# The gated delta rule of a two-block kernel, its 16-blocks inverted by a recurrence on VectorE instead of squarings on TensorE, both head halves phase by phase

## The chip, the cores and the metric

One Trainium2 chip, one core of it. The metric is the device time of one launch in microseconds (us). TensorE, VectorE, ScalarE, GpSimd and SyncE appear in the rows as PE (its weight loads as PEld), DVE, ACT, POOL and SP (the queue of DMA issues as SPq). All data are fp32.

## The reference, cut to what matters

Two blocks run one after the other. The first (dilated attention, a convolution branch, memory attention, then a mixture of 32 experts over 256 tokens) matters here only through its experts, whose 192 MB of weights are read once. The second block projects 256 context tokens and 256 latent tokens, runs a state space scan (SSD) and a gated delta rule over both, in two directions, and ends in a feed-forward layer. The change is in the delta rule:

```python
def gdn_chunk_scan(q, k, v, log_a, beta, s0):
    """S_t = a_t (I - b_t k_t k_t^T) S_{t-1} + b_t k_t v_t^T, o_t = S_t^T q_t, chunked (WY form)."""
    g = jnp.cumsum(log_a, axis=2)
    diff = g[:, :, :, None] - g[:, :, None, :]
    a_mat = einsum("bclhd,bcshd->bclsh", k, k) * beta * masked_exp(diff, strict)
    lhs = a_mat + eye
    rhs = concatenate([v * beta, k * (beta * exp(g))], -1)
    u, w = split(triangular_solve(lhs, rhs, lower=True, unit_diagonal=True))
    qk = einsum("bclhd,bcshd->bchls", q, k) * masked_exp(diff, incl)
    def step(s, inp):
        v_new = u_c - w_c @ s
        o = (q * exp(g)) @ s + qk_c @ v_new
        s = s * dec_c + kd_c^T @ v_new          # kd = k * exp(g_last - g)
        return s, o
```

There are 8 heads of 128 channels. The kernel takes chunks of 128 tokens, so there are 2 chunks of context and 2 latent ones, in each direction: 8 chunk steps, and in each a 128x128 unit triangular matrix I + A per head has to be inverted.

## The kernel before, in words

**Stages.** The first block's attention part ends some 430 us into the span. Then the experts run (to some 1045 us), and on the same engines, woven in by a planned order, the second block's context part: its channels (projection, convolution), `ssd0` to `ssd3`, and the delta rule's context steps m = 0 to 3. After that come the latent channels, the SSD steps with the gate projections (some 1190 to 1299 us), the delta rule's latent steps m = 4 to 7 (`LATENT`, some 1297 to 1526 us), and the output projection and the feed-forward layer.

**The planner.** `context_phases` lists the context's phases with a cost each, `expert_phases` those of the experts, and `mixed_schedule` (L128) spreads the context's evenly over the experts' phases, in proportion to the costs (272.8 in all). Each engine's program is written in this order: an instruction of a later phase never passes one of an earlier phase on the same engine. The expert weights stream through a ring of 6 slots of 1 MB, issued by SP, which waits until the unit that held a slot has been used.

**One delta step before** (`gdn_pe` L561, `gdn_act` L941, `gdn_dve` L1174, `gdn_pool` L1523). The 8 heads are two halves h of 4. A "four" (L567 to L572) is one group of 4 fp32 products of 128x128x128 into one PSUM bank, written as 8 matmul instructions; `transposes` (L1966, the matmul at L1970) does 4 transposes the same way. In each phase the loop `for h in range(2)` does both halves:

- rows: transposes of k (gkT) and, as a four, the cumulated decay along the rows (gR); DVE clips the difference (L1190), ACT takes exp (L958, L961), POOL multiplies with the triangular mask (L1539, L1542);
- gram: k k^T (gKK, and on the latent side gQK); DVE multiplies (L1203) and cuts out minus the 16x16 diagonal blocks N (L1180); POOL adds the identity (L1547);
- AT: A transposed. P2, X2, X4, X8: (I + N)(I + N^2)(I + N^4)(I + N^8) by squarings, 8 fours per half, copied out of PSUM by ACT (L949) or added by DVE (L1222);
- three levels (blocks of 32, 64, 128): XT, T and Y, a transpose and two fours per half each, with POOL's masked copy of A (L1535) and DVE's subtraction (L1232);
- w (only where there is a state), v (L662, L664) and S: the state's part, the new values, outputs and the state.

**Around it.** `second_block_pe` (L797 to L809) puts the modulation products `mod_part` (L2123) and `mod_sum` (L785) and the sums `q_sums` (L792) between the phases; DVE does `modulate` (L1382), and after step 4 `gated_y` (L1390), after 5 `normed_y` (L1401). In the SSD steps the decays along rows come from fours (ssd_rows, L752), 4 per step.

## Time and profile before

| | before |
|---|---|
| runs | 1863.32, 1867.92, 1871.38 us; median 1867.92 |
| the profiled execution | 1869.31 us, its span 1867.6 us |
| PE busy | 1708.2 us (91%), mean granted clock 0.956 |
| DVE, ACT, POOL busy | 684.6, 435.7, 213.2 us |
| DMA | 372.69 MB, 200 GB/s over the span |

The span runs from the first to the last instruction of the profiled execution; its own time is 1.7 us longer. An engine's busy time counts neither its waits nor its semaphore instructions. TensorE's granted clock is a share of 2.4 GHz.

### The profile page before, as it was taken

How to read it: one execution, taken by the hardware profiler on the slowest of the kernel's cores; microseconds unless marked ns; L12 is line 12 of the kernel's file. 1: busy time of each engine (PE TensorE's matmuls, PEld its weight loads, DVE VectorE, ACT ScalarE, POOL GpSimd, SP SyncE). 2: the span in 40 equal slices, each digit the busy share in tenths (PEclk: the TensorE clock that was granted, in tenths of full speed). 3: DMA queues.
4: the chain of work that ended last, by engine and by line, in shares of the span. 5: the costliest groups of instructions: out<-in, count | busy, mean ns of one | idle time of the engine just before them, and what ended most of it. 6: DMA issues, size and time to landing. Idle time of an engine off the chain costs nothing.

```text
span 1867.6 us, 25449 instructions
## 1 busy us (share of the span) xinstructions
PE 1708.2 (91%) x10656; PEld 1209.9 (65%) x10656; DVE 684.6 (37%) x1404; ACT 435.7 (23%) x889; POOL 213.2 (11%) x190
## 2 busy tenths in 40 slices
PE   7999999999888879999999899899989989699996
PEld 3558555456666547767766588666978874488842
DVE  2107113335434353323233377665355450400003
ACT  1010454013111123323332231322333430000000
POOL 2000000020000012221212100011342320100000
PEclk9999999998988889999999899999999999799998
DMA  7444335723999888979989434224121222244340
GB/s 242 163 148 143 128 125 190 251 103 135 372 394 350 326 317 343 416 318 365 415 340 393 171 137 148 90 91 176 62 91 46 91 91 90 90 138 178 123 155 38
DMA packets 124295, 372.69 MB, mean 200 GB/s; under 512 B 10523, under 2 KB 26517, under 8 KB 107413
## 3 DMA queue, kind: packets, MB, share of 16 engines
q1 hardware_dynamic: 118245, 361.12, 51.6%
q0 software_dynamic: 1568, 8.39, 1.2%
q10 hardware_dynamic: 4368, 1.54, 0.4%
q8 instruction: 87, 1.43, 0.3%
q14 instruction: 27, 0.22, 0.0%
HBM read 369.98 MB, written 1.05 MB: 199 GB/s over the span
## 4 chain that ended last, share of the span: by engine, by line
PE 77%; DMA 13%; DVE 7%; ACT 1%; issue 1%; SPq 0%; DVEq 0%; ACTq 0%
PE psum L1976 49%; PE psum L571 10%; DMA ring<-in_w_down 4%; PE psum L1775 4%; DMA ring<-in_w_up 4%; DMA ring<-in_w_in 4%; PE psum L1970 3%; PE psum L1816 2%; PE psum L1759 2%; PE psum L1797 1%; PE psum L2093 1%; PE psum L768 1%; PE psum L2123 1%; PE psum L557 1%; DVE area L1180 1%
## 5 line engine op out<-in xcount | busy, mean ns | idle before, releaser
L1976 PE MATMUL psum<-area,ring 128*128 128x256 f32 x1984 | 457.7, 391 | 15.1 <-DMA ring<-in_w_in 14.1
L1976 PE MATMUL psum<-ring,area 128*128 128x512 f32 (+1 forms) x1040 | 452.5, 595 | 8.6 <-DMA ring<-in_w_proj_mem 2.4
L1976 PEld LDWEIGHTS psum<-area,ring 128*128 128x128 f32 x1984 | 386.1, 197 | 75.2 <-DMA ring<-in_w_in 18.1
L1976 PEld LDWEIGHTS psum<-ring,area 128*128 128x128 f32 x1040 | 198.9, 193 | 252.7 <-issue 251.7
L571 PEld LDWEIGHTS psum<-area 128*128 128x128 f32 x2304 | 269.7, 194 | 34.7 <-issue 19.1
L571 PE MATMUL psum<-area 128*128 128x128 f32 x2304 | 281.0, 280 | 10.6 <-DVE area L1180 10.4
L949 ACT ACTIVATE area<-psum 128x512 f32<-128x512 f32 x236 | 138.7, 597 | 243.7 <-PE psum L571 127.8
L2249 ACT ACTIVATE area<-psum 128x512 f32<-128x512 f32 x116 | 66.4, 599 | 460.9 <-PE psum L1976 362.2
L1970 PE MATMUL psum<-const,area 128*128 128x128 f32 x736 | 120.6, 294 | 52.0 <-DVE area L1490 14.8
L1970 PEld LDWEIGHTS psum<-const,area 128*128 128x128 f32 x736 | 90.5, 149 | 97.4 <-issue 23.0
L1775 PE MATMUL psum<-ring,area 128*32 128x256 f32 x2048 | 124.8, 388 | 12.5 <-DMA ring<-in_w_up 12.3
L1775 PEld LDWEIGHTS psum<-ring,area 128*32 128x32 f32 x2048 | 64.0, 111 | 59.3 <-issue 24.0
L1144 DVE SCALAR_TENSOR_TENSOR area<-area,cols 128x268 f32<-128x268 f32 (+1 forms) x186 | 91.6, 492 | 6.6
L1797 PE MATMUL psum<-ring,area 128*32 128x256 f32 x1024 | 68.2, 398 | 19.8 <-DMA ring<-in_w_down 19.4
L1535 POOL TENSOR_TENSOR area<-area,const 128x512 f32<-128x512 f32 x48 | 60.1, 1274 | 219.2 <-PE psum L571 219.2
L913 ACT COPY area<-psum 128x256 f32<-128x256 f32 x62 | 23.1, 373 | 210.6 <-PE psum L1976 210.6
L1142 DVE TENSOR_SCALAR area<-area,cols 128x268 f32<-128x268 f32 (+1 forms) x62 | 22.1, 356 | 120.3 <-ACT area L913 119.1
L1514 POOL TENSOR_TENSOR area<-area 128x1024 f32<-128x1024 f32 x4 | 10.8, 2728 | 461.9 <-DVE area L2371 461.9
L1797 PEld LDWEIGHTS psum<-ring,area 128*32 128x32 f32 x1024 | 31.0, 113 | 50.0 <-DMA ring<-in_w_down 22.0
L1501 DVE TENSOR_TENSOR area<-psum,area 128x512 f32<-128x512 f32 x11 | 7.6, 691 | 151.5 <-PE psum L1976 151.5
L1232 DVE TENSOR_TENSOR area<-area,psum 128x512 f32<-128x512 f32 x48 | 32.9, 687 | 67.2 <-PE psum L571 67.1
L1222 DVE TENSOR_TENSOR area<-psum,area 128x512 f32<-128x512 f32 x48 | 33.2, 691 | 60.7 <-PE psum L571 60.2
(304 smaller groups left out, 1346.5 us busy)
## 6 DMA issues: line engine op xcount, KB each, us to landing
ring<-in_w_gate SPq DMA_DIRECT2D x64, 1024.0 KB, 9.6
ring<-in_w_up SPq DMA_DIRECT2D x64, 1024.0 KB, 11.5
ring<-in_w_down SPq DMA_DIRECT2D x64, 1024.0 KB, 11.3
ring<-in_w_in SPq DMA_DIRECT2D x29, 2048.0 KB, 8.4
ring<-in_w_ada SPq DMA_DIRECT2D x12, 2048.0 KB, 8.1
ring<-in_w_in SPq DMA_DIRECT2D x13, 1024.0 KB, 7.5
ring<-in_w_out SPq DMA_DIRECT2D x6, 2048.0 KB, 8.5
ring<-in_w_ffn_gate SPq DMA_DIRECT2D x5, 2048.0 KB, 7.8
```

What stands on the lines that cost most here:

```text
L571: last = nc.tensor.matmul(dst[:, i * P:(i + 1) * P], lhs(i), rhs(i), start=True, stop=True)
L949: nc.scalar.activation(dst, src, ACT.Copy, scale=scale).then_inc(drain_of(key), 1)
L1144: link(v.scalar_tensor_tensor(dst, src, w, dst, ALU.mult, ALU.add))
L1222: v.tensor_tensor(bb[h][7], four(key), bb[h][7], ALU.add).then_inc(drain_of(key), 1)
L1535: g.tensor_tensor(b[6], b[3], by_row(LEVELS[lev]), ALU.mult).then_inc(s["level_ready"], 1)
L1759: last = nc.tensor.matmul(dst[:, j * P:(j + 1) * P], h2[:, t, k * P:(k + 1) * P], place[:, t, q * P:(q + 1) * P], start=t == 0, stop=t == ...
L1775: last = nc.tensor.matmul(wide.dst[CAP * j:CAP * (j + 1), 0:2 * P], hcT[:, q % 2, k, rows], both[:, :, k % 4, j * P:(j + 1) * P], start=k ...
L1797: last = nc.tensor.matmul(dst[CAP * g:CAP * (g + 1), 0:256], actT_e[:, e % 2, CAP * j:CAP * (j + 1)], w[:, j % 2, g * 256:(g + 1) * 256], ...
L1816: nc.tensor.matmul(dst, placeT[:, q, t * P:(t + 1) * P], y_quad[:, q % 2, half * WIDE:(half + 1) * WIDE], start=True, stop=True).then_inc( ...
L1970: last = nc.tensor.transpose(t[0:width, j * P:j * P + rows], src, ident[0:rows, 0:rows])
L1976: last = nc.tensor.matmul(dst, lhs(k), rhs(k), start=first and k == 0, stop=final and k == count - 1)
L2249: nc.scalar.activation(dst, src, func).then_inc(drain_of(key), 1)
```

## The change

Each half h is now a stream of its own (`gdn_pe(pe, m, h, ...)` and so on), and `staggered` weaves the two streams on every engine: with `STAGGER = 0` each phase of half 1 is followed at once by the same phase of half 0, which is emitted with it. The squarings go. In their place:

- compact (DVE): cut the 16x16 diagonal blocks out of A, fold them to 16 columns, spread them over (row, column) pairs;
- rep (PE, ACT): two products with the block mask, each with 512 columns, give each token all 256 entries of its own block for every head; ACT copies them out;
- solve (DVE): a recurrence of 15 steps, each a multiplication and a subtraction on 4 heads x n elements, n from 15 to 1, each instruction waiting for the one before; then four multiplications write the block-diagonal inverse, transposed, into XT;
- X0, Y0, X1, Y1, X2, Y2: one transpose and two fours per level as before, in two phases instead of three. AT is gone, since XT is kept transposed;
- where there is a state, w goes: k S (gK) is taken beside X2, scaled by ACT in 4 instructions and subtracted from beta v on DVE, and v is one four;
- gR, and ssd_rows of the SSD, are now transposes of the cumulated decay, not fours;
- the planner's costs are new (226.6 in all), and so is the place of the hooks for the modulation and the sums.

With the new costs the planner starts `rows 0` after `gate_up_b 14` (before: after `gate_up_a 12`), and the other steps after `down 17`, `down 21` and `turn 26` (before: `turn 16`, `down 20`, `gate_up_a 26`). Between `rep` and `X0` of both halves there stand, in the four context steps, `gate_up_b, down, turn`; `down, turn, gate_up_a`; `turn, gate_up_a, gate_up_b`; and `gate_up_a, gate_up_b`. Between `gram` and `rep` there are two of the experts' phases each time: `turn, gate_up_a`; `gate_up_a, gate_up_b`; `gate_up_b, down`; and `down, turn`.

```diff
 CTX_GAP = 3
+STAGGER = 0
...
+def staggered(first, second):
+
+    for _ in range(STAGGER):
+        yield "0 " + next(first)
+    while True:
+        phases = [("1 ", next(second, None)), ("0 ", next(first, None))]
+        if phases[0][1] is None:
+            return
+        for half, phase in phases:
+            if phase is not None:
+                yield half + phase
+
+
...
 
-    gdn = [("rows", 3.1), ("gram", 1.9), ("AT", 1.2), ("P2", 3.8), ("X2", 5.7), ("X4", 3.8), ("X8", 1.9), ("XT0", 1.2),
-           ("T0", 1.9), ("Y0", 1.9), ("XT1", 1.2), ("T1", 1.9), ("Y1", 1.9), ("XT2", 1.2), ("T2", 1.9), ("Y2", 1.9),
-           ("w", 1.9), ("v", 2.9), ("S", 1.9)]
+    costs = {"rows": 1.2, "gram": 1.0, "compact": 0.5, "rep": 1.8, "solve": 0.5, "X0": 1.6, "Y0": 1.0, "X1": 1.6, "Y1": 1.0,
+             "X2": 2.1, "Y2": 1.0, "v": 1.0, "S": 1.0}
...
+    half = [f"{name} {m}" for m in range(4) for name in costs]
+    return phases + [(phase, costs[phase.split()[1]]) for phase in staggered(iter(half), iter(half))]
...
+        def delta_half(h, wide, spread_at, columns, small_at):
+            triangle, keys, block, decay = [place + 512 * h for place in columns]
...
+                 [delta_half(h, 8192, 10240, (16000, 17024, 25216, 26240), 15360) for h in range(2)]]
+        unit_16 = stats[:, 24:40]
...
+            transposes(("gkT", m, h), [k_gdn[side][:, t, head * P:(head + 1) * P] for head in heads])
+            transposes(("gR", m, h), [cum[side][:, d, t, 16 + head:17 + head].to_broadcast([P, P]) for head in heads])
...
+            yield "compact"
+            pe.wait_ge(s["spread_ready"], 2 * m + h + 1)
+            for i in range(2):
+                pair = slice(2 * i, 2 * i + 2)
+                nc.tensor.matmul(open_tile(("gRep", m, h, i)), blk16, b["spread"][:, pair, :, :].rearrange("p h i j -> p (h i j)"),
+                                 start=True, stop=True).then_inc(filled, 1)
+            yield "rep"
+            yield "solve"
...
+                if lev == 0:
+                    pe.wait_ge(s["XT_ready"], 2 * m + h + 1)
+                else:
+                    wait_drained(pe, ("gY", m, h, lev - 1))
+                transposes(("gX", m, h, lev), [b["XT"][:, i, :] for i in range(4)])
+                pe.wait_ge(s[f"levels_{h}"], 3 * m + lev + 1)
+                four(("gV", m, h, lev), lambda i: b["AL"][:, i, :], lambda i: b["XT"][:, i, :])
+                if ci and lev == 2:
+                    wait_drained(pe, ("gS", m - 2, h))
+                    four(("gK", m, h), lambda i: b["kT"][:, i, :], lambda i: state[:, 4 * h + i, :])
+                yield f"X{lev}"
+                wait_drained(pe, ("gX", m, h, lev))
+                wait_drained(pe, ("gV", m, h, lev))
+                four(("gY", m, h, lev), lambda i: b["X"][:, i, :], lambda i: b["VT"][:, i, :])
...
+            wait_drained(pe, ("gY", m, h, 2))
             if ci:
...
+                pe.wait_ge(s["r_ready"], 2 * (m - 2) + h + 1)
+            else:
+                pe.wait_ge(s["kv_ready"], 2 * m + h + 1)
+            four(("gv", m, h), lambda i: b["XT"][:, i, :], lambda i: b["A"][:, i, :])
...
+        def gdn_steps(steps, half):
+
+            def of_half(h):
+                for m in steps:
+                    for phase in half(m, h):
+                        yield f"{phase} {m}"
+
+            return staggered(of_half(0), of_half(1))
...
                     dst = open_tile(("ssd_rows", m, q))
                     for j in range(4):
-                        last = nc.tensor.matmul(dst[:, j * P:(j + 1) * P],
-                                                log_a[1][:, c - 2, d, 4 * q + j:4 * q + j + 1].to_broadcast([P, P]),
-                                                (upto, since)[d], start=True, stop=True)
+                        last = nc.tensor.transpose(dst[:, j * P:(j + 1) * P],
+                                                   cum[1][:, d, c - 2, 4 * q + j:4 * q + j + 1].to_broadcast([P, P]), ident)
                     last.then_inc(filled, 1)
...
+            for phase in gdn_steps(LATENT, lambda m, h: gdn_pe(pe, m, h, open_tile, transposes)):
+                half, phase, m = phase[0], phase[2:-2], int(phase[-1])
                 tile = MOD_FIRST + 2 * (m - 4)
-                for phase in gdn_pe(pe, m, open_tile, transposes):
+                if half == "0":
                     if phase == "gram":
                         mod_part(tile)
-                    if phase == "AT":
+                    if phase == "rep":
                         mod_sum(tile)
-                    if phase == "X8":
+                    if phase == "X0":
                         mod_part(tile + 1)
-                    if phase == "T1":
+                    if phase == "X2":
                         mod_sum(tile + 1)
-                if m in (5, 6):
...
+            for i in range(2):
+                key = ("gRep", m, h, i)
+                nc.scalar.copy(b["rep"][:, 2 * i:2 * i + 2, :, :].rearrange("p h i j -> p (h i j)"),
+                               wait_filled(eng, key)).then_inc(drain_of(key), 1)
...
-            yield "AT"
-            yield "P2"
-            for name in ("X2", "X4", "X8"):
-                for h in range(2):
-                    key = ("g" + name, m, h)
-                    v.tensor_tensor(bb[h][7], four(key), bb[h][7], ALU.add).then_inc(drain_of(key), 1)
-                yield name
-            yield "XT0"
+            wait_drained(eng, ("gKK", m, h))
+            block, rows = b["block"], b["rows"]
+            link(v.tensor_tensor(block, b["A"], blk16.unsqueeze(1).to_broadcast([P, 4, P]), ALU.mult))
+            link(v.tensor_reduce(rows, block.rearrange("p h (g j) -> p h j g", j=16), AX.X, ALU.add))
+            for i in range(4):
+                ins = v.tensor_tensor(b["spread"][:, i, :, :], rows[:, i, :].unsqueeze(1).to_broadcast([P, 16, 16]),
+                                      unit_16.unsqueeze(2).to_broadcast([P, 16, 16]), ALU.mult)
+            ins.then_inc(s["spread_ready"], 1)
+            yield "compact"
+            yield "rep"
+            rep, Y, tmp = b["rep"], b["Y"], b["step"]
+            link(v.tensor_copy(Y, unit_16.unsqueeze(1).to_broadcast([P, 4, 16])))
+            for i in range(2):
+                wait_drained(eng, ("gRep", m, h, i))
+            for j in (range(15), range(15, 0, -1))[d]:
+                left = (slice(j + 1, 16), slice(0, j))[d]
+                n = left.stop - left.start
+                link(v.tensor_tensor(tmp[:, :, 0:n], rep[:, :, left, j], Y[:, :, j:j + 1].to_broadcast([P, 4, n]), ALU.mult))
+                link(v.tensor_tensor(Y[:, :, left], Y[:, :, left], tmp[:, :, 0:n], ALU.subtract))
+            XT = b["XT"]
+            for i in range(4):
+                ins = v.tensor_tensor(b["XT"][:, i, :].rearrange("p (g j) -> p g j", j=16),
+                                      Y[:, i, :].unsqueeze(1).to_broadcast([P, 8, 16]),
+                                      blk16.rearrange("p (g j) -> p g j", j=16), ALU.mult)
+            ins.then_inc(s["XT_ready"], 1)
+            yield "solve"
             for lev in range(3):
-                yield f"T{lev}"
-                for h in range(2):
-                    key = ("gY", m, h, lev)
-                    if lev == 2:
-                        wait_drained(eng, ("gXT", m, h, lev))
-                    dst = bb[h][7 if lev < 2 else 4]
-                    v.tensor_tensor(dst, dst, four(key), ALU.subtract).then_inc(drain_of(key), 1)
+                yield f"X{lev}"
+                key = ("gY", m, h, lev)
+                v.tensor_tensor(XT, XT, four(key), ALU.subtract).then_inc(drain_of(key), 1)
+                if ci and lev == 2:
+                    wait_drained(eng, ("gK", m, h))
+                    eng.wait_ge(s["kv_ready"], 2 * m + h + 1)
+                    v.tensor_tensor(b["A"], b["A"], b["AL"], ALU.subtract).then_inc(s["r_ready"], 1)
                 yield f"Y{lev}"
-                if lev < 2:
-                    yield f"XT{lev + 1}"
-            if ci:
...
+                wait_filled(eng, ("gRep", m, h, 1) if lev == 0 else ("gV", m, h, lev - 1))
+                g.tensor_tensor(b["AL"], b["A"], by_row(LEVELS[lev]), ALU.mult).then_inc(s[f"levels_{h}"], 1)
```

## Rows read from the trace of the kernel before

**Rows 1.** the page: busy time of each engine over the span.

```profile
PE 1708.2 (91%) x10656; PEld 1209.9 (65%) x10656; DVE 684.6 (37%) x1404; ACT 435.7 (23%) x889; POOL 213.2 (11%) x190
```

**Rows 2.** the page: the chain that ended last, by engine.

```profile
PE 77%; DMA 13%; DVE 7%; ACT 1%; issue 1%; SPq 0%; DVEq 0%; ACTq 0%
```

**Rows 3.** busy us by stretch, four experts in each, beside context steps.

```profile
core 0: us, PE busy (x) PEld busy (x) DVE busy (x) ACT busy (x) POOL busy (x), PEclk, DMA share, GB/s
722.20:792.20 70.00, 65.99 (x711) 50.09 (x710) 25.22 (x49) 23.37 (x46) 17.40 (x14) 0.98 0.92 372
792.20:859.40 67.20, 63.12 (x703) 48.17 (x702) 18.64 (x35) 19.40 (x40) 11.56 (x10) 1.00 0.86 349
859.40:927.30 67.90, 65.25 (x718) 49.58 (x718) 21.76 (x46) 23.18 (x47) 20.21 (x16) 1.00 0.95 380
927.30:998.00 70.70, 66.75 (x734) 51.63 (x733) 23.68 (x51) 23.96 (x46) 14.41 (x11) 1.00 0.91 365
sum 275.80, PE 261.11 PEld 199.48 DVE 89.31 ACT 89.92 POOL 63.59; mean PE 65.28 PEld 49.87 DVE 22.33 ACT 22.48 POOL 15.90
```

**Rows 4.** two stretches of 10 us among the experts, columns as above.

```profile
750.00:760.00 10.00, 10.00 (x127) 7.46 (x129) 2.52 (x5) 4.34 (x10) 5.88 (x6) 1.00 1.02 418
800.00:810.00 10.00, 10.00 (x139) 7.58 (x138) 1.73 (x5) 2.70 (x6) 0.00 (x0) 1.00 0.24 78
```

**Rows 5.** the two parts of latent step 5, columns as above.

```profile
1357.84:1368.70 10.86, 3.86 (x10) 1.97 (x10) 10.86 (x31) 4.19 (x7) 7.81 (x6) 0.69 0.57 194
1368.70:1411.60 42.90, 42.39 (x362) 39.55 (x362) 13.57 (x21) 17.46 (x29) 15.89 (x13) 1.00 0.15 50
```

**Rows 6.** the page, groups: busy us, mean ns | idle before, releaser.

```profile
L571 PE MATMUL psum<-area 128*128 128x128 f32 x2304 | 281.0, 280 | 10.6 <-DVE area L1180 10.4
...
L1232 DVE TENSOR_TENSOR area<-area,psum 128x512 f32<-128x512 f32 x48 | 32.9, 687 | 67.2 <-PE psum L571 67.1
```

**Rows 7.** timeline of PE among the experts: start us, us, engine, line.

```profile
732.74 1.93 PE L1775 MATMUL psum<-ring,area 128*32 128x256 f32 x32
734.61 2.05 PE L571 MATMUL psum<-area 128*128 128x128 f32 x16
...
745.17 0.66 PE L1970 MATMUL psum<-const,area 128*128 128x128 f32 x4
...
792.05 3.74 PE L1759 MATMUL psum<-area 128*128 128x128 f32 x32
795.62 3.60 PE L1816 MATMUL psum<-area 128*128 128x512 f32 x8
```

**Rows 8.** timeline of latent step 5, clips to gram, columns as above.

```profile
1357.84 4.22 DVE L1190 TENSOR_SCALAR area<-psum,area 128x128 f32<-128x128 f32 x16
...
1359.69 2.49 POOL L1539 TENSOR_TENSOR area<-area,const 128x512 f32<-128x512 f32 x2 [18.54 <-ACT area L958]
...
1361.97 2.15 DVE L1203 SCALAR_TENSOR_TENSOR area<-psum,area 128x128 f32<-128x128 f32 x8
...
1363.14 2.15 PE L1970 MATMUL psum<-const,area 128*128 128x128 f32 x8 [5.38 <-DVE area L1203]
...
1365.09 1.92 PE L785 MATMUL psum<-area 128*128 128x512 f32 x2
```

**Rows 9.** timeline of DVE in the router, a chain of linked small instructions.

```profile
424.10 0.17 DVE L2639 TENSOR_TENSOR area<-area,r_prio 128x16 f32<-128x16 f32 x1
424.30 0.17 DVE L2640 TENSOR_REDUCE area<-area 128x2 f32<-128x16 f32 x1
...
432.77 0.23 DVE L2684 SCALAR_TENSOR_TENSOR area<-area 128x64 f32<-128x64 f32 x1
```

**Rows 10.** a group of DVE by shape: busy us, mean ns | idle before.

```profile
L2541 DVE TENSOR_TENSOR area<-area 128x256 f32<-128x256 f32 x6 | 2.5, 424 | 0.2
```

**Rows 11.** line L752, the SSD decays: ns min/median/max.

```profile
L752 PE MATMUL psum<-const,area x128: 275/275/276, 1187.7 to 1274.5; 128*128 128x128 f32 x128
```

**Rows 12.** line L1180 of DVE: ns min/median/max.

```profile
L1180 DVE SCALAR_TENSOR_TENSOR area<-area,const x32: 677/684/1774, 705.8 to 1485.7; 128x512 f32<-128x512 f32 x32
```

More of the change, by code:

```diff
@@ L1570, in gdn_pool @@
[L1570 to L1578 removed]
+            yield "compact"
+            yield "rep"
+            wait_drained(eng, ("gKK", m, h))
@@ L1597, in context_pool @@
                 yield f"ssd{m}"
[L1598 to L1600 removed]
+            for phase in gdn_steps(range(4), lambda m, h: gdn_pool(eng, g, m, h)):
+                yield phase
         def experts_pool():
```

450 lines of the change are left out of this document (153 added, 297 removed).

## The prediction, made before the changed kernel was run

> **What bounds the kernel now.** I read the page first: PE is busy nine tenths of the span [rows 1], and PE makes up 77% of the chain that ended last, DMA 13%, DVE 7% [rows 2]. So removed products count only where nothing else then ends last. The delta rule runs in two places.
>
> Among the experts, four experts and about one context step take 70.0, 67.2, 67.9 and 70.7 us, 275.8 together; PE is busy 261.1 of them and the DMA share is 0.86 to 0.95 [rows 3]. In a 10 us stretch the DMA moves 418 GB/s where it is never held up, and 78 GB/s beside a gather and scatter, where PE uses no weights [rows 4]. Four experts are 4 x 6 units of 1 MB, 25.2 MB, or 60.2 us at 418 GB/s. Both resources are close: PE ends last, but 4 x 60.2 = 241 us is the floor that no saving on PE goes below, 35 us under today's 276.
>
> On the latent side nothing streams worth speaking of. Step 5 has two parts: 10.9 us in which DVE is busy throughout and PE for 3.9, then 42.9 us in which PE is busy for 42.4 [rows 5]. From the first clip to the last product of S that is 53.8 us.
>
> **What leaves PE.** A four costs 0.89 us (1.95 us for 16 instructions with the first one's latency, 280 ns each before overlap [rows 6]; two fours stand as 2.05, two gathers' worth of 32 instructions as 3.74 [rows 7]). A group of transposes costs 0.55 in a row of them (0.66 alone [rows 7]). Per half, a context step has 18 fours (20 with a state) and 5 groups of transposes; afterwards 9 (10), 5 groups (gR takes AT's place) and the two 512-column products of rep. Such a product stands as 1.02 us alone (two instructions, 1.92 at the low clock [rows 8]); in a row I take 0.90 each, 1.8 per half, nearly two fours. Net 7 (8) fours, 6.2 (7.1) us per half, so 12.5, 12.5, 14.2 and 14.2 us per context step: **53 us less PE work among the experts**. The same on the latent side.
>
> **What DVE adds.** All of it is in series with PE, because X0 of a half waits for its XT.
> - compact, per half: a multiplication and a fold over 512 elements (0.69 each [rows 6]) and four multiplications of 256 (424 ns alone [rows 10], about 1.47 for four back to back): 2.9 us.
> - solve, per half: 30 linked instructions on 4 to 60 elements, 32 on average. A linked pair on 16 elements starts 0.20 us apart and 64 elements take 0.23 [rows 9]; I take 0.22, between them, and keep 0.20 and 0.26 as ends. 30 x 0.22 = 6.6, a copy 0.2, four multiplications into XT 1.1 (as 16 clips of 128 take 4.22 [rows 8]): 7.9 us (7.3 to 9.1).
> - Both halves: 5.8 us of compact and 16.0 us (waits included) of solve per step, in place of squarings that PE did while ACT and DVE followed at 0.3 us.
>
> **The latent steps.** STAGGER is 0, so between rep and X0 PE has nothing of the other half; only `mod_sum` stands there. From the first clip: clips 4.2, then gram of half 1 (1.1 and 0.6), gram of half 0 when POOL's masks (1.25 each, now A, QK, A, QK [rows 8]) let it: 7.7 us. Compact to 13.5. Rep and its copies of half 1 are done by then. Solve of half 1 to 21.6, of half 0 to 29.6. X0 of half 1 is hidden in this, that of half 0 is not. After it PE runs: X0 1.4, mod_part 1.9, Y0 1.8, X1 2.9, Y1 1.8, X2 with gK 4.7, mod_sum 1.0, Y2 1.8, two subtractions exposed 1.0 (0.69 each [rows 6]), v 3.6, S 3.6: 25.5, in all 55.1 against 53.8, **+1.3 us per step** at full clock. But after its 5 us of idleness at 1357.84 the granted clock of that stretch is 0.69 [rows 5] and the next products come at 1.92 instead of 1.02 us [rows 8]: that is the lower of the two levels, 1.2 GHz. Now PE is idle for about 6 us before rep and some 12 of the 16 us of solve, so I let rep (which pushes solve by 1.2) and X0 with mod_part (+1.4 and +1) run at that level: +3.6, less 0.9 for what step 5 already loses so today. **+4 per step, +16 us for four** (low end 4 x 1.3 = 5; high end 4 x 5 = 20, with 0.26 per link 30).
>
> Work of DVE between the steps (gated_y, normed_y, the sums) stays where it was and costs the same. The hooks on half 1's X0 stand where DVE waits for Y0 anyhow; if that cover went, `o_squares` would cost 3 us once.
>
> **The context steps.** Per step PE waits twice. At rep: DVE needs 2.1 + 2.9 us for half 1 and 2.9 more for half 0, the experts' phases in between fill 2 to 4 us (1.93 each [rows 7]): about 3 us of waiting. At X0: between rep's end and X0 three phases fill about 4 us; solve of half 1 ends 7 us after rep, of half 0 another 8 later; X0 of half 1 is 1.5 of it: 3 + 6.7 = 9.7 us of waiting. Together 12.8 us, and 1.5 for restarting at the low clock: 14.3 x 4 = 57 us. Behind solve on DVE stands the experts' multiplication out of PSUM, and behind that on PE the turn and `down`, and behind those SP's loads: it costs no more as long as PE waits at X0 anyway. The ring holds 6 MB, 15 us at 418 GB/s, so DMA goes on during such a wait and takes 5 of the 14.7 us (275.8 - 261.1 [rows 3]) that PE waits today. Where the planner puts phases sums to nothing: the channels spread over more experts, the delta steps are denser later. **-53 + 57 - 5 = -1 us.** The bounds are far: -25 if the waits fall where PE would wait for weights, +25 if all that PE idles today stays and links cost 0.26.
>
> **The SSD steps.** 16 fours of L752 (275 ns, 128 instructions [rows 11]) become transposes, 16 x 0.34 = **-5 us**, since PE is the busy one there; 0 if DVE ends last instead.
>
> gK's scaling on ACT, POOL's products and the reduction into unit_16 cost nothing: each runs while PE or DVE is busy with the other half; without that cover gK's four activations would cost 1.2 us in each of four steps.
>
> **The sum.** -1 - 5 + 16 = +10 us. Against the profiled execution's 1869.3 that is 1879.3; the median stands 1.4 lower, so 1878.
>
> **The rivals.**
> 1. *The experts gain after all* (0.31), the other side. Place: the stretches of rows 3. Price: a wait at X0 costs nothing while PE would soon stand before an empty ring. For it: weights land late at many points even now, and DMA has 35 us to give. Against: PE waits only 14.7 us there today. It decides once the waits per step are under about 8 us: then the experts' part gains 25, the latent steps with their low end cost 8: 1869 - 25 - 5 + 8 = 1847, less the 1.4: 1846.
> 2. *It comes out even* (0.08): the clock is kept through solve, latent +5, nothing among the experts: 1868.
> 3. *POOL in DVE's way* (0.09). The clearest row is L1180: two SBUF inputs, 684 ns as a rule, 1774 at most, beside POOL's masks [rows 12]. All of solve's instructions have two SBUF inputs, and POOL's level masks for both halves run as soon as rep is filled, 1.25 us each, beside compact of half 0 and solve of half 1. If they exclude each other that is 2.5 us per step, 8 x 2.5 = 20 us: 1898. The Trainium skill states such a rule ("SBUF — State Buffer", Who interferes with whom): a VectorE instruction with two inputs in SBUF and a GpSimd instruction that reads SBUF take the shared read port by turns, each for its whole length. By that rule, which the stretched row agrees with, rival 3 would be the right size or a bit under it.
> 4. *The ring starves* (0.05): DVE late for the experts, waits beyond the ring's 15 us: another 30 us, 1908.
> The forecast keeps 0.47; its own range is 1862 to 1898.
>
> **The numbers.** 0.5% is 9.3 us, about what this kernel's measurements can tell. Faster by more: rival 1 but for 0.04, 0.27. Slower by more: the forecast but for 0.07, and rivals 3 and 4, 0.54. Within: 0.19. The range runs from rival 1 to rival 4.
>
> **What would show it.** Right: PE idle before X0's transposes, put down to DVE, 7 to 10 us per step among the experts and 6 + 7 us on the latent side; a granted clock well under 1 there; steps 4 to 6 from clip to S near 58 us; the four stretches near 69 us still. Wrong: stretches near 62 us and a DMA share near 1 (rival 1); links 0.3 us apart or more beside POOL (rival 3); DVE's solve much shorter than 7.9 us per half, in which case all of this shrinks.

## The result, and the profile after

| | before | after |
|---|---|---|
| median (range), runs | 1865.62 us (1862.92 to 1871.38), 4 | 1980.87 us (1977.35 to 1985.16), 4 |
| ratio after / before | | 1.0614, 95% interval 1.0577 to 1.0651 |
| span of the profiled execution | 1867.6 us | 1977.0 us |
| mean granted clock | 0.956 | 0.914 |

The change costs 6.1%. The forecast had the sign, and a tenth of the size. Of the page after, first the busy times [rows 1], the chain [rows 2], and the groups that wait most [rows 6]:

```profile
PE 1610.7 (81%) x9408; PEld 1093.7 (55%) x9408; DVE 797.9 (40%) x1993; ACT 402.6 (20%) x862; POOL 174.9 (9%) x162
...
PE 68%; DVE 15%; DMA 10%; ACT 3%; issue 2%; POOL 1%; SPq 0%; DVEq 0%; ACTq 0%; POOLq 0%
...
L1909 PE MATMUL psum<-const,area 128*128 128x128 f32 x736 | 125.6, 302 | 156.7 <-DVE area L1186 119.0
L592 PE MATMUL psum<-area 128*128 128x128 f32 x1408 | 192.2, 293 | 27.0 <-ACT area L923 19.9
...
L608 PE MATMUL psum<-area,const 128*128 128x512 f32 x64 | 47.7, 915 | 59.6 <-DVE area L1170 59.6
```

PE is busy 97.5 us less (111 were expected: 53, 53 and 5), DVE 113.3 more, and DVE's share of the chain has doubled. PE stands 119.0 us before X0's transposes (L1909, released by the writes into XT, L1186) and 59.6 before rep (L608, released by compact's last multiplication, L1170).

**Where the time went.** Three marks that both kernels have cut the span: the first of the latent channel products (the experts' end), the first clip of latent step 4, and the first output product after step 7. Busy us of each engine from the first gather (L1759 before, L1698 in the changed kernel) to the experts' end, and over the latent steps, before:

```profile
core 0: us, PE busy (x) PEld busy (x) DVE busy (x) ACT busy (x) POOL busy (x), PEclk, DMA share, GB/s
438.24:1061.14 622.90, 553.27 (x5328) 400.57 (x5326) 228.55 (x479) 166.99 (x377) 87.42 (x64) 0.94 0.88 345
1295.58:1542.73 247.15, 219.80 (x1791) 196.42 (x1791) 127.31 (x245) 93.79 (x158) 88.45 (x74) 0.96 0.25 91
```

and after, the same columns, with the three stretches of four experts that answer to those of [rows 3]:

```profile
434.86:1112.90 678.04, 507.74 (x4752) 347.56 (x4750) 285.25 (x771) 151.02 (x358) 68.24 (x52) 0.88 0.80 317
1344.31:1653.52 309.21, 179.08 (x1191) 143.38 (x1190) 183.57 (x541) 77.54 (x152) 69.25 (x58) 0.80 0.20 74
...
708.23:804.77 96.54, 62.43 (x586) 39.77 (x584) 49.10 (x138) 21.49 (x40) 19.46 (x14) 0.84 0.62 247
804.77:888.91 84.14, 60.41 (x622) 42.38 (x621) 37.95 (x123) 20.59 (x41) 14.20 (x12) 0.86 0.75 299
888.91:969.15 80.24, 61.76 (x638) 44.21 (x637) 39.35 (x123) 22.29 (x47) 14.23 (x12) 0.89 0.85 335
```

The span's +109.4 us are: experts' end 1112.9 against 1061.1, **+51.8**; from there to the first latent clip 231.4 against 234.4, **-3.0** (the SSD's part); the latent steps, **+62.1**; the rest **-1.4**. (From the first gather on the experts' part is 55.1 longer; it starts 3.4 earlier.) Among the experts PE's busy time fell by 45.5 and its idle time rose by 100.7 (69.6 to 170.3); on the latent side busy fell by 40.7 and idle rose by 102.8 (27.4 to 130.1). The forecast had 52 (57 - 5) and 69 (16 + 53): so the rise is twice as large among the experts and half as large again on the latent side.

**What PE waits for.** Latent step 6, clip at 1423.53, the timeline of after: start us, us, engine, line, in brackets the idle time before it and its releaser.

```profile
1423.53 4.22 DVE L1146 TENSOR_SCALAR area<-psum,area 128x128 f32<-128x128 f32 x16
1426.74 0.63 ACT L930 ACTIVATE area<-area 128x512 f32<-128x512 f32 x1 [10.33 <-DVE area L1146]
...
1428.42 3.58 PE L592 MATMUL psum<-area 128*128 128x128 f32 x16 [9.53 <-ACT area L923]
...
1439.33 0.68 DVE L1167 TENSOR_TENSOR area<-area,const 128x512 f32<-128x512 f32 x1
1440.05 1.00 DVE L1168 TENSOR_REDUCE area<-area 128x64 f32<-128x512 f32 x1
1441.08 1.43 DVE L1170 TENSOR_TENSOR area<-area,stats 128x256 f32<-128x256 f32 x4
...
1442.57 6.73 PE L608 MATMUL psum<-area,const 128*128 128x512 f32 x8 [8.72 <-DVE area L1170]
...
1449.45 1.26 POOL L1495 TENSOR_TENSOR area<-area,const 128x512 f32<-128x512 f32 x1 [1.69 <-PE psum L608]
1449.46 1.32 DVE L1183 TENSOR_TENSOR area<-area 128x48 f32<-128x48 f32 x1
1450.81 0.23 DVE L1182 TENSOR_TENSOR area<-area 128x44 f32<-128x44 f32 x1
1451.07 0.20 DVE L1183 TENSOR_TENSOR area<-area 128x44 f32<-128x44 f32 x1
...
1455.73 0.90 DVE L1186 TENSOR_TENSOR area<-area,const 128x128 f32<-128x128 f32 x4
...
1463.80 0.90 DVE L1186 TENSOR_TENSOR area<-area,const 128x128 f32<-128x128 f32 x4
...
1464.75 1.11 PE L1909 MATMUL psum<-const,area 128*128 128x128 f32 x4 [14.59 <-DVE area L1186]
```

Half 1 has its spread at 1439.4, but rep of half 1 begins at 1442.57, when half 0 has its own too. Half 1 has its XT at 1456.6, but its X0 begins at 1464.75, when half 0's is done. The exp of half 1 (L930) starts when half 0's first four clips are done too. PE has nothing of one half to do beside the other's solve. The code gives a reason: the waits on signals (semaphores) that both halves share count `2 * m + h + 1` (L605, for one), the value at which half 0 and then half 1 have signalled; `staggered` emits half 1 first, and its wait for `2 * m + 2` is met only by half 0. Twelve waits have this form. That is a reading of code and rows; the first two runs below test it.

The links, the small instructions of solve that wait for one another, run as forecast where nothing disturbs them (0.17 to 0.25 us each, starts 0.20 to 0.28 apart).

### The profile page after: what moved, and what is told of

It is laid out like the page before. It is cut to its first block, busy times and chain, and to the rows that moved or that the text cites. A ratio compares the mean times of both kernels' runs of the same rounds, so it can differ in the third digit from the quotient of the medians.

```text
span 1977.0 us, 23427 instructions
## 1 busy us (share of the span) xinstructions
PE 1610.7 (81%) x9408; PEld 1093.7 (55%) x9408; DVE 797.9 (40%) x1993; ACT 402.6 (20%) x862; POOL 174.9 (9%) x162
## 3 DMA queue, kind: packets, MB, share of 16 engines
q8 instruction: 77, 1.26, 0.3%
## 4 chain that ended last, share of the span: by engine, by line
PE 68%; DVE 15%; DMA 10%; ACT 3%; issue 2%; POOL 1%; SPq 0%; DVEq 0%; ACTq 0%; POOLq 0%
PE psum L1915 45%; PE psum L592 7%; PE psum L1909 3%; PE psum L1714 3%; DMA ring<-in_w_up 3%; DMA ring<-in_w_in 3%; DMA ring<-in_w_down 3%; DVE area L1182 3%; DVE area L1183 3%; PE psum L608 2%; PE psum L1736 2%; PE psum L1755 1%; PE psum L1698 1%; DVE area L1170 1%; POOL area L1498 1%
## 5 line engine op out<-in xcount | busy, mean ns | idle before, releaser
L1915 PE MATMUL psum<-area,ring 128*128 128x256 f32 x1984 | 448.5, 386 | 10.3 <-DMA ring<-in_w_in 9.3
L1909 PE MATMUL psum<-const,area 128*128 128x128 f32 x736 | 125.6, 302 | 156.7 <-DVE area L1186 119.0
L592 PE MATMUL psum<-area 128*128 128x128 f32 x1408 | 192.2, 293 | 27.0 <-ACT area L923 19.9
L1909 PEld LDWEIGHTS psum<-const,area 128*128 128x128 f32 x736 | 96.9, 155 | 197.2 <-DVE area L1186 123.9
L592 PEld LDWEIGHTS psum<-area 128*128 128x128 f32 x1408 | 181.7, 207 | 43.3 <-issue 22.1
L2188 ACT ACTIVATE area<-psum 128x512 f32<-128x512 f32 x116 | 66.4, 599 | 455.4 <-PE psum L1915 359.5
L923 ACT COPY area<-psum 128x512 f32<-128x512 f32 x128 | 73.4, 588 | 231.8 <-PE psum L1909 168.6
L1714 PEld LDWEIGHTS psum<-ring,area 128*32 128x32 f32 x2048 | 67.3, 115 | 84.8 <-issue 52.2
L608 PE MATMUL psum<-area,const 128*128 128x512 f32 x64 | 47.7, 915 | 59.6 <-DVE area L1170 59.6
L1495 POOL TENSOR_TENSOR area<-area,const 128x512 f32<-128x512 f32 x48 | 61.2, 1274 | 313.0 <-PE psum L592 199.8
L1463 DVE TENSOR_TENSOR area<-psum,area 128x512 f32<-128x512 f32 x11 | 7.6, 692 | 151.0 <-PE psum L1915 151.0
L608 PEld LDWEIGHTS psum<-area,const 128*128 128x128 f32 x64 | 18.4, 303 | 87.0 <-DVE area L1170 64.9
L1182 DVE TENSOR_TENSOR area<-area 128x60 f32<-128x60 f32 (+14 forms) x240 | 52.7, 220 | 33.4 <-ACT area L939 25.4
L1194 DVE TENSOR_TENSOR area<-area,psum 128x512 f32<-128x512 f32 x48 | 32.9, 687 | 69.5 <-PE psum L592 68.8
```

The lines of the kernel that those rows point to most:

```text
L592: last = nc.tensor.matmul(dst[:, i * P:(i + 1) * P], lhs(i), rhs(i), start=True, stop=True)
L608: nc.tensor.matmul(open_tile(("gRep", m, h, i)), blk16, b["spread"][:, pair, :, :].rearrange("p h i j -> p (h i j)"), start=True, stop=Tru ...
L923: nc.scalar.copy(dst, src).then_inc(drain_of(key), 1)
L1182: link(v.tensor_tensor(tmp[:, :, 0:n], rep[:, :, left, j], Y[:, :, j:j + 1].to_broadcast([P, 4, n]), ALU.mult))
L1495: g.tensor_tensor(b["AL"], b["A"], by_row(LEVELS[lev]), ALU.mult).then_inc(s[f"levels_{h}"], 1)
L1714: last = nc.tensor.matmul(wide.dst[CAP * j:CAP * (j + 1), 0:2 * P], hcT[:, q % 2, k, rows], both[:, :, k % 4, j * P:(j + 1) * P], start=k ...
```

## The experiments

All ratios are to the kernel before, run beside each kernel on the same chip. Differences in us are of medians of different sets of runs, between which before's own median moved from 1864.83 to 1869.33; so they are good to some 5 us, and where that matters the ratios are compared too. "Solve" and "rep" are the phases, "after" is the changed kernel, and "the swapped order" the first run.

**1 and 2. The order of the halves, and the counts.** The first swaps what `staggered` emits, the second leaves it and makes the waits count in the order of emission, in 12 places:

```diff
-        phases = [("1 ", next(second, None)), ("0 ", next(first, None))]
+        phases = [("0 ", next(first, None)), ("1 ", next(second, None))]
```
```diff
-            pe.wait_ge(s["spread_ready"], 2 * m + h + 1)
+            pe.wait_ge(s["spread_ready"], 2 * m + 2 - h)
```

> The changed kernel with half 0 emitted ahead of half 1 in every phase (one line of `staggered`). Theory A: the waits count 2m+h+1, as if half 0 signalled first; with half 1 emitted first, half 1's waits ask for both halves (2m+2), so rep, X0 and the masks of half 1 wait for half 0's work too. Then this order lets the first half go ahead: in the latent steps gram is done some 5 us earlier, rep of the first half 3 us earlier and X0 of it is hidden in the second solve: clip to S falls from 70.6 us to 57 to 60, and the wait before X0 among the experts from 17 to about 10. Whole kernel 1895 to 1925 us. Rival B (length of the recurrence and low clock alone, order indifferent): within 8 us of the changed kernel's 1981.

> The changed kernel, half 1 still first, but the twelve waits of the form 2m+h+1 count in the order of emission (2m+2-h). Theory A: the same gain as with half 0 first, within 8 us of that run, 1895 to 1925 us, since only the counts coupled the halves. Rival B: 1981 within 8. If the order itself matters (hooks, POOL's order) and not the counts, this stays near 1981 while the other order gains.

Measured: 1923.05 us, ratio 1.0277 (1.0245 to 1.0309), and 1924.57 us, ratio 1.0298 (1.0251 to 1.0345). Two different edits, one effect: 56 to 58 us of the 115 by the medians, 59 to 63 by the ratios. In the first, PE's waits from 430 to 1620 us (in total, how often, the longest), and latent step 5:

```profile
PE psum L1909 <- DVE area L1186: 95.4, 16, 9.2
PE psum L608 <- DVE area L1170: 28.3, 11, 4.3
```
```profile
1417.22 1.88 PE L758 MATMUL psum<-area 128*128 128x512 f32 x2
1423.57 1.11 PE L1909 MATMUL psum<-const,area 128*128 128x128 f32 x4 [4.47 <-DVE area L1186]
...
1432.72 1.12 PE L1909 MATMUL psum<-const,area 128*128 128x128 f32 x4 [6.33 <-DVE area L1186]
```

X0 now waits 16 times (once per half and step) and at most 9.2 us, instead of 8 times and at most 17.3 in after; X0 of half 0 starts 9.15 us before that of half 1, beside its solve. Latent falls from 309.2 to 268.6 us, the experts' end from 1112.9 to 1099.4. The coupling is shown, and it is mostly a matter of the latent side. The rest of the runs build on the swapped order where not said otherwise.

**3 and 9. A short solve.** One of the recurrence's 15 steps is left, so the inverted blocks aren't those of the reference; the third run has after's order, the ninth the swapped one.

```diff
-            for j in (range(15), range(15, 0, -1))[d]:
+            for j in (range(14, 15), range(1, 0, -1))[d]:
```

> The changed kernel with 1 of the 15 steps of the recurrence left in each solve (the other 14 are left out, so the block inverses are not the reference's). 28 linked DVE instructions, 6.2 us, less per half, 16 halves: 100 us less on DVE. If solve is exposed in full: 1981 - 100 = 1881. Where the ring or the experts' weights would have ended last among the experts, less comes back there: the latent half (8 halves) 50 us, the experts' part 30 to 50: 1881 to 1901. If the coupling and not the length of solve were the whole of the loss: under 40 us gained.

> Half 0 first, as in the run that changed only that, and 1 of the recurrence's 15 steps left, so the inverted blocks are not those of the reference. About 12.5 us of DVE per half-pair and step go, 100 us in all. Theory A (with the halves uncoupled, solve's length is still what PE stands for): PE's waits at X0, 95 us, nearly vanish; experts lose most of the 52 us that context steps wait, latent falls from 268.6 to some 225: 1830 to 1850, below before. Theory B (what is left of the loss sits in the low clock, in compact and in the order of the phases): the waits move to other places, and it stays at 1865 or above.

Measured: 1874.22 us, ratio 1.0025 (1.0001 to 1.0049), so 107 under after; and 1816.50 us, ratio 0.9723 (0.9674 to 0.9773), 107 under the swapped order. The ninth kernel's stretches, first gather to experts' end and latent:

```profile
435.38:1051.40 616.02, 507.02 (x4752) 342.79 (x4750) 241.57 (x547) 150.58 (x358) 68.35 (x52) 0.91 0.88 349
1283.54:1489.99 206.45, 164.13 (x1192) 131.80 (x1190) 138.29 (x317) 78.36 (x152) 70.49 (x58) 0.93 0.30 110
```

Against the swapped order DVE is busy 102 us less (810.8 to 708.9). Solve's length, the gaps between its links included, falls by 117, from 145 us in all to 28, half of it in each part. The time falls by 107 us by the medians, with the halves coupled or not (110 with them coupled and 103 without by the ratios): by 62.2 on the latent side, but by 48.0 among the experts, where waits for weights take back a part (the section on the prediction has the rows). So nearly the whole length of solve was exposed. Both runs came out below what was expected of them. With next to no solve the new form would be 2.8% faster than before, and most of that is latent (206.5 us instead of 247.2); the experts' part, 616.0 instead of 622.9, gains 6.9 us of the 46 by which PE's busy time fell.

**4 and 5. The low clock.** Products whose result nobody reads keep PE busy before rep and X0: in the fourth run on after's latent side alone, in the fifth in all steps of the swapped order.

```diff
                         mod_sum(tile)
+                        for _ in range(13):
+                            nc.tensor.matmul(psum[:, 6, :], ones, const[:, 0:4, :].rearrange("p a n -> p (a n)"), start=True, stop=True)
```

(and 5 of them behind `mod_part` in the fourth run; in the fifth 1 and 2 before rep of half 0 and 1, and 4 and 6 before X0).

> The changed kernel with extra products on constants in PE's idle time of the latent steps: 5 of 512 columns before rep (after mod_part), 13 between rep and X0 (after mod_sum); results unused. Clock theory: rep (6.7 us at the low level for four products) falls towards 4 and X0 to Y0 lose their 2 to 3 us: 4 to 5 us per step, 1961 to 1965 in all. Rival: the idle time was never worth more than 1 us per step, 1977 to 1981. If the extra products run into X0, up to 10 us slower.

> The kernel with half 0 first, and extra products of 512 columns on constants in the PSUM bank that is written next: 1 and 2 before rep, 4 and 6 before X0 of half 0 and 1, in all eight steps (results overwritten). They stand where PE waits for DVE. Clock theory: between gathers PE is busy 61 to 62 us where before it was 65 with some 13 us more work, so the low level costs 8 to 9 us per step among the experts and 3 on the latent side; kept at the full level that comes back: 1923 - 30 = 1893 (range 1880 to 1905). Rival (the waits cost by their length alone, and the extra products only get in the way where the wait is short): 1920 to 1935.

Measured: 1983.92 us, ratio 1.0592 (1.0551 to 1.0634), the latent part 308.5 us, no gain; and 1914.55 us, ratio 1.0264 (1.0236 to 1.0291), 8.5 under the swapped order. The fourth kernel's step 6:

```profile
1449.47 5.21 PE L608 MATMUL psum<-area,const 128*128 128x512 f32 x8 [4.07 <-DVE area L1176]
1454.51 1.02 PE L758 MATMUL psum<-area 128*128 128x512 f32 x2
1455.38 11.32 PE L783 MATMUL psum<-const 128*128 128x512 f32 x26
1471.20 1.11 PE L1915 MATMUL psum<-const,area 128*128 128x128 f32 x4 [4.51 <-DVE area L1192]
```

Rep shrank from 6.73 to 5.21 us, but the idle products (L783) ended 4.5 us early and X0 ran at the lower level all the same, so this run says nothing of X0. The fifth does: its stretches of four experts stand at a granted clock of 0.92, 0.96 and 1.00 (the swapped order's 0.87, 0.89, 0.89), its latent part at 0.92 instead of 0.82. The gain is small and uncertain: 8.5 us by the medians, about 2 by the ratios, whose intervals overlap, 11.4 by the profiled spans (the experts' end is 10.0 earlier, the latent part 3.2 shorter). So holding the clock in this way gives back 2 to 11 us, not the 30 that were expected. What the low clock costs by itself isn't separated, since the idle products can also hold up PE's own work (run 12).

**6. The planner's cost of solve**, 6.3 instead of 0.5, so that more of the experts' phases stand between rep and X0.

> The kernel with half 0 first and the planner's cost of solve 6.3 instead of 0.5 per half, so that the context's total is as large as before and some six of the experts' phases stand between solve and X0. If PE's wait for XT among the experts (about 10 us per step) is a matter of too little work beside it, it goes, and the channels are as dense as before: 1923 - 25 to 35 = 1888 to 1898. Rival: the experts' multiplication stands behind solve on DVE, in order, so PE stops at the experts' turn instead of at X0: 1910 to 1930, with the wait moved to other lines.

Measured: 1901.08 us, ratio 1.0190 (1.0161 to 1.0218), 22 us under the swapped order by the medians, 16 by the ratios, and all of it among the experts (end at 1074.5, latent 268.5). PE's wait at X0 fell from 95.4 to 46.8 us, which is the latent side's alone; part of it came back elsewhere, for DVE works in order: the experts' turn waits 20.2 us for DVE's multiplication (L1865), which is written behind a solve.

**7. The transposes alone**: the kernel before with gR and ssd_rows as transposes.

> The kernel before with one part of the change alone: gR and ssd_rows as transposes of the cumulated decay. The prediction's term: 5 us less in the SSD steps, 0.3 us per half in the delta steps, where gR runs under DVE's work: 1869 - 5 = 1864 (0.3% faster), and 1859 if gR's saving among the experts counts too. Rival: nothing, DVE ends last there: ratio 1.000.

Measured: 1862.44 us, ratio 0.9981 (0.9963 to 0.9998), 2.4 us faster; the part from the experts' end to the first latent clip is 232.4 instead of 234.4.

**8. Half 0 six phases ahead**, `STAGGER = 6` in after; this also puts the signals into the order that the counts ask for.

> The changed kernel with STAGGER 6 instead of 0: half 0 is six phases ahead of half 1, so the solve of one half stands beside v, S, rows and gram or X0 to Y2 of the other, and half 0 signals first, as the counts ask. If the loss is that PE has nothing of its own beside solve: PE's wait for XT (119 us) goes to under 40, latent part from 309 to 230 us or less, whole kernel 1981 - 57 (order) - 60 = 1850 to 1875. If the recurrence's own length on DVE or the shorter runs of products at the low clock bound it anyway: 1890 to 1920.

Measured: 1913.53 us, ratio 1.0258 (1.0232 to 1.0284). That is the second of the two cases expected: PE's wait at X0 is 77.6 us, where under 40 had stood for the first. The experts' end is 1074.7, 25 us better than with the swapped order, but latent takes 281.3, 12.7 more: there both halves' phases alternate on engines that work in order, and a new wait appears (L1909 on the subtraction L1194, 12.3 us).

**10. What helped, together**: half 0 first, six ahead in the context only, cost 6.3, idle products.

> Everything that helped in one kernel: half 0 first, in the context half 0 runs six phases ahead (on the latent side not), the planner's cost of solve 6.3, and idle products ahead of rep and X0 that hold the clock. Theory A (the experts' part loses by solves that are not covered by enough of the experts' phases): each half's solve has two to four of the experts' phases for itself; the experts' end comes at 1063 to 1070, latent stays at about 265: 1880 to 1890. Theory B (more interleaving brings more in-order waits, as the six phases ahead did on the latent side): the experts' end at 1075 or later, 1893 or more. Neither expects it to beat before, since latent alone is 18 us longer.

Measured: 1896.87 us, ratio 1.0152 (1.0099 to 1.0205). The experts' end is at 1072.9, hardly earlier than with the costs alone (1074.5), and the total is what theory B had. Why the gains don't add is not shown: the idle products are in this kernel too, and run 12 shows that they can cost more than they bring.

**11 and 12. One chain for both halves.** Since solve's length is what is paid, shorten it: the recurrence of both halves in the same 30 instructions, planner's cost 4.0. The twelfth adds idle products.

```diff
-            rep, Y, tmp = b["rep"], b["Y"], b["step"]
+            if h == 0:
+                rep, Y, tmp = [at(place, 8, *shape) for place, shape in joint_at[side]]
...
-                link(v.tensor_tensor(tmp[:, :, 0:n], rep[:, :, left, j], Y[:, :, j:j + 1].to_broadcast([P, 4, n]), ALU.mult))
+                    link(v.tensor_tensor(tmp[:, :, 0:n], rep[:, :, left, j], Y[:, :, j:j + 1].to_broadcast([P, 8, n]), ALU.mult))
```

> Half 0 first, and the recurrence of both halves in one chain: 30 linked instructions on 8 heads x n elements instead of 60 on 4 x n, in the phase solve of half 0; the planner's cost of solve is 4.0. A link on 4 to 60 elements is mostly fixed time (0.17 to 0.25 us busy), so one on 8 to 120 should start some 0.24 us after the one before: 7.2 us and 2.3 for the writes into XT, 9.8 us per step in place of 16.5. Theory A (solve's length is exposed nearly one to one, as the run with 1 of 15 steps showed): latent 240 to 250, the experts' end 1058 to 1068, together 1850 to 1872, so about even with before or better. Theory B (what is won is lost since X0 of half 0 can no longer run beside solve of half 1, and the experts' multiplication stands behind one long solve): 1880 or more.

> As e11_joint, with idle products of 512 columns ahead of rep (1 and 2) and 6 ahead of X0 of half 0, all steps, which hold the granted clock. Theory A (the low clock after the wait for solve still costs 1 to 2 us per step, as in the run of this kind before, -8.5 us): 5 to 9 us under e11_joint. Theory B (among the experts, where the wait for solve is now covered, the idle products are themselves in the way, 5.6 us of PE per step): latent some 4 us shorter, the experts' part as much or more longer, no gain in all.

Measured: 1874.53 us, ratio 1.0035 (1.0017 to 1.0053), 48.5 under the swapped order; and 1890.06 us, ratio 1.0122 (1.0099 to 1.0146). The eleventh kernel's links and its step 5:

```profile
1381.32 0.28 DVE L1186 TENSOR_TENSOR area<-area 128x120 f32<-128x120 f32 x1
1381.63 0.34 DVE L1185 TENSOR_TENSOR area<-area 128x112 f32<-128x112 f32 x1
...
1389.05 0.17 DVE L1186 TENSOR_TENSOR area<-area 128x8 f32<-128x8 f32 x1
1389.26 1.71 DVE L1189 TENSOR_TENSOR area<-area,const 128x128 f32<-128x128 f32 x8
1390.21 1.12 PE L1913 MATMUL psum<-const,area 128*128 128x128 f32 x4 [9.48 <-DVE area L1189]
```

Twice the elements cost a subtraction 0.28 instead of 0.22 us at the long end and nothing (0.17) at the short one; undisturbed, the 30 links take 8.3 us instead of 7.0. From the first link (1380.48) to the last write solve takes 10.5 us for both halves instead of 17 to 19. Latent is 250.6 us (247.2 before), the experts' end 1064.6 (1061.1); in all the run lies just above what theory A had (1850 to 1872). Idle products are in the way once PE has work of its own there: +15.5 us in the twelfth run, nearly all of it among the experts (end at 1080.4).

**13 and 14. Cover.** The joint form with 1.5 and with 6.5 as the planner's cost of solve.

> As e11_joint with the planner's cost of solve 1.5 instead of 4.0, so two of the experts' phases stand between rep of half 1 and X0 of half 0 instead of four or five. Theory A (what is left of the experts' loss is too little cover over solve): the experts' end 6 to 15 us later than e11_joint's 1064.6, 1880 to 1890. Theory B (it is the channels, pushed together ahead of the delta steps, whose loads keep the DMA full): the experts' end earlier or the same, 1868 to 1875.

> As e11_joint with the planner's cost of solve 6.5: six or seven of the experts' phases stand between rep and X0. Theory A (cover is what lacks): the experts' end 3 to 6 us earlier than 1064.6, 1867 to 1872. Theory B (channels pushed together): later, 1878 or more. In both, the latent part stays at 250 to 251.

Measured: 1875.65 us, ratio 1.0049 (1.0020 to 1.0077), and 1866.57 us, ratio 0.9997 (0.9978 to 1.0016). So a cost of 6.5 instead of 4.0 is worth 8 us, as theory A had it, but 1.5 costs hardly anything (the experts' end is 1059.1 in its profile, one of its fastest executions, against the eleventh's 1064.6), where theory A had it 6 to 15 us later. Cover alone doesn't explain all three. The fourteenth kernel, which is even with before:

```profile
438.35:1055.69 617.34, 499.23 (x4752) 337.75 (x4750) 264.40 (x647) 149.11 (x357) 68.14 (x52) 0.92 0.88 348
1289.65:1542.21 252.56, 174.20 (x1192) 139.50 (x1190) 164.25 (x417) 78.46 (x152) 69.61 (x58) 0.86 0.25 90
```

Here the experts' part is 5.6 us shorter than before, where the work saved on PE is 54, and the latent part 5.4 longer. No complete form of the recurrence that was run beats before; the seventh kernel, which has none, does by 0.2%.

## Why the prediction was wrong

**Right.** The side, and the mechanism: PE idle before rep and X0, put down to DVE. The PE work: predicted 53 and 53 less; where the clock is least disturbed it is 54 among the experts (553.3 to 499.2, the fourteenth run) and 56 latent (219.8 to 164.1, the ninth). The links start 0.23 us apart where 0.22 was forecast, and an undisturbed solve takes 8.2 us per half (7.9), compact 3.2 (2.9). The latent steps, once the halves are independent: +16 us predicted for four, +21.5 measured (268.6 against 247.2). The transposes of the SSD: -5 predicted, -2 to -3 measured, so something else, DVE by the forecast's lower end, ends last in part of these steps.

**The step that failed first** is in the latent steps: "Rep and its copies of half 1 are done by then. Solve of half 1 to 21.6 ... X0 of half 1 is hidden in this". It follows each half by its own data, and never asks which value the waits count to. Written so that half 1 comes first, each half's rep and X0 wait for both. Step 6, from its first clip to its last product of S, took 70.6 us where 55 to 58 were forecast: solve of half 0 was done after 41.2 us, not 29.6, and what follows took 29.4, not 25.5. Runs 1 and 2 put it at 57 us by the medians; by the profiled spans it is 54, of them 40.6 of the latent part's 62.1 and 13.5 of the experts' 51.8. The rows before can't show this; the diff does.

**The second** is in the sum of the context steps, -53 + 57 - 5 = -1. Against it stand 51.8, or 38.3 with the coupling gone. Term by term in the swapped order: PE's busy time from the first gather to the experts' end fell by 35.8 (553.3 to 517.5), not 53; the number of products is the same as in the fourteenth run, where it fell by 54 at a higher granted clock (0.92 against 0.87), so the rest of the saving went into products at the low clock. Waits at X0 and rep in the context steps were 60.9 us (49.1 and 11.8, the whole span's less the latent part's 46.3 and 16.5), for which 12.8 x 4 = 51 had stood. And the waits for weights did not shrink by 5: over the experts' part they grew by 17.4, from 45.8 to 63.2. That last term is the one furthest off.

Where they grew is not where the prediction looked, which was the four stretches of experts beside delta steps. Here are PE's waits for weights up to the fifth gather, before (438.24 to 722.10) and in the swapped order (435.57 to 712.20), in total, how often, the longest:

```profile
PE psum L1797 <- DMA ring<-in_w_down: 14.4, 12, 2.8
PE psum L1976 <- DMA ring<-in_w_in: 14.1, 8, 3.3
...
PE psum L1775 <- DMA ring<-in_w_up: 3.7, 3, 1.6
```
```profile
PE psum L1714 <- DMA ring<-in_w_up: 25.7, 10, 4.9
PE psum L1736 <- DMA ring<-in_w_down: 15.2, 9, 3.1
PE psum L1915 <- DMA ring<-in_w_in: 7.2, 6, 1.8
```

That is 48.1 us instead of 32.2, and no delta step has begun there yet in the swapped order: its first clip is at 737.7, before's was at 698.0. The DMA moves the same 97 MB or so in both (340 and 350 GB/s over 283.9 and 276.6 us), PE is busy 18.5 us less (239.6 to 221.1), and 15.9 of them come back as waits for weights. Behind that gather such waits are 15.1 us, before 13.6. "DMA goes on during such a wait" held: the ninth run, whose delta steps hardly stall PE (3.3 us at X0), waits longer for weights there, 28.1 us. And "Where the planner puts phases sums to nothing" holds for the sum of these waits, not for their place: run 6, whose costs put the first clip back to 696.0, has 32.9 us ahead of the fifth gather and 27.1 behind it. Over the whole experts' part the runs 1, 6, 9, 11 and 14 all stand at 60 to 73 us of waits for weights, the ninth highest, against 45.8 before. So the step that failed is the term of the weights: it took 5 us off them and counted the 53 of PE in full, where less work on PE beside the same weights means more waiting for them, stall or no stall. In the ninth run, with hardly any wait at X0, PE's busy time falls by 46.3 and 27.3 of it are waits for weights again.

**Exposure.** In the swapped order PE's idle time is still 76.7 us above before's among the experts (146.3 to 69.6) and 58.2 on the latent side (85.6 to 27.4): 135, beside the 201 us that compact and solve take in eight steps there (3.2 to 4.3 per compact and half, 17 to 19 per step for solve). About two thirds of the length that DVE got in series with PE show as idle time, and the ninth run says that shortening solve by 117 us gives back 107. The forecast knew this chain's length, less the collisions with POOL below, and had 121 us of idle time for it (52 and 69).

**The rivals.** The experts gain (0.31): no. The fourteenth run gains 5.6 us there with both halves in one chain and cover planned for it, the ninth 6.9 with next to no solve; 25 had been priced, so with less waiting at X0 the saved work still went mostly into waits for weights. POOL in DVE's way (0.09): it is there. Row 1449.46 shows it, a link of 48 elements that took 1.32 us instead of 0.21 and ended as POOL's mask (1449.45 + 1.26) did. Twelve of solve's instructions in after take over 0.15 us more than the median of their shape, 8.8 us in all; measured by the same medians it is 21 of solve's and compact's in the swapped order, 20.6 us in all, each beside one of POOL's level masks (L1495), and that is the size that the rival had. The rule of the Trainium skill ("SBUF — State Buffer", Who interferes with whom) agrees with these rows: the two take turns, each for its whole length. No run moved the masks, so what they cost the kernel is not shown beyond DVE's own time. The ring starves (0.05): not beyond its 15 us during a stall; the waits for weights that grew are those told above. The low clock: forecast at 1.5 us per context step and 2.7 net per latent one, 17 in all; holding it gave back 2 to 11 (run 5).

**Open.** How the 38 us of the experts' part split between the cover of solve and the place of the delta steps is only bounded: the planner's costs move both at once, by 25 us in run 6 and by 8 between runs 11 and 14. The copies of k behind the exps on ACT (L923, 13.7 us of PE's waiting in the swapped order) were not tried in another order. That PE's smaller work is what brings the waits for weights is the reading that fits all of these rows; no run changed the loads themselves.

## What to carry to other kernels

Where two streams share a semaphore, its counts fix an order of the streams; read it out of the wait's value and hold it against the order of emission, before any timeline is drawn. A chain of small linked instructions costs mostly its number of links (twice the elements made these 30 a fifth longer): put independent chains into one before hiding any of them. Where an engine at 90% hands work to another in series with it, add up the new chain's whole length first, and count a cover only for work that is written between the two on every engine in question. Where weights stream close to their limit, work taken off the engine that uses them comes back as waits for them, in places that the change never touched.

## What the runs showed of the chip

- A link of DVE on 4 elements takes 0.17 us and on 8 too; on 60, 0.25 (a multiplication) or 0.22 (a subtraction), on 112, 0.34 (a multiplication). The next one starts 0.03 to 0.04 us after its end.
- PE fell to the lower level (1.2 GHz) again after 4.5 us of idleness that followed 17 us of unbroken work (run 4): X0's products took 1.11 and 1.91 us, against 0.66 and 1.06 later in the step. Rep's 8 instructions took 6.73 us in step 6 of after (0.84 each), where 4 in a row took 1.98 in run 1 (0.50 each, at 830.37 for one): mostly the lower level's time.
- The fold (L1168), a reduction of 512 elements to 64, takes 1.01 us, where a multiplication on as many takes 0.68.
- A link that meets one of POOL's masks lasts until the mask ends: 1.13 to 1.36 us instead of 0.2, in 14 of the 480 links of run 1.
